# A router with the weights as the stationary side, and the norm's weight applied after the gather

## The reference, cut to what matters

```python
xn = rms_norm(h, ffn_norm_g)
group_prob = softmax(xn @ w_rg + b_rg)                  # 4 groups
g_w, g_idx = top_k(group_prob, 1)
e_logits = (xn @ w_re + b_re).reshape(B, S, 4, 8)       # 32 experts
sel = e_logits of the chosen group
e_w, e_idx = top_k(softmax(sel), 2); e_w = e_w / sum(e_w)
cw = one-hot of the two experts, times g_w * e_w         # S x 32
out = sum over e of (silu(xn @ w_gate[e]) * (xn @ w_up[e]) * cw[:, e]) @ w_down[e]
h = h + out; return rms_norm(h, final_norm_g)
```

## Time and profile before

| | us | share of the span |
|---|---|---|
| median of three runs | 1063.31 | |
| the profiled execution | 1062.29 | |
| its span | 1060.5 | |
| TensorE matmuls busy | 983.5 | 93% |
| TensorE weight loads busy | 752.2 | 71% |
| VectorE busy | 543.3 | 51% |
| ScalarE busy | 471.3 | 44% |
| GpSimd (POOL) busy | 8.0 | 1% |

### The profile page before, as it was taken

The page is one execution under the profiler, slowest core; times in us unless marked ns, Lnnn a source line. Parts: engine busy times, 40 slices in busy tenths (PEclk is TensorE's granted clock), DMA queues, the critical chain, the costliest instruction groups (busy, mean ns, idle before and its releaser), DMA issues.

```text
span 1060.5 us, 13681 instructions
## 1 busy us (share of the span) xinstructions
PE 983.5 (93%) x5518; PEld 752.2 (71%) x5518; DVE 543.3 (51%) x870; ACT 471.3 (44%) x753; POOL 8.0 (1%) x10
## 2 busy tenths in 40 slices
PE   5999998989999999999998879998948999999995
PEld 5879886877889999888887657797745444554542
DVE  4788785664666554555776654664361111111114
ACT  5488656555455344445554635353332222222222
POOL 0000000000000000000000000000020000000000
PEclk9999999999999999999999989999958999999998
DMA  9655464333554555436564423381564999999991
GB/s 297 233 165 179 134 237 161 118 119 121 192 175 159 200 197 190 168 122 208 171 194 129 170 80 120 123 313 47 169 228 178 383 393 395 394 393 396 393 367 42
DMA packets 106740, 224.02 MB, mean 211 GB/s; under 512 B 10041, under 2 KB 13874, under 8 KB 106674
## 3 DMA queue, kind: packets, MB, share of 16 engines
q1 hardware_dynamic: 103936, 218.13, 58.9%
q10 hardware_dynamic: 2738, 4.96, 1.4%
HBM read 222.03 MB, written 1.05 MB: 210 GB/s over the span
## 4 chain that ended last, share of the span: by engine, by line
PE 77%; DVE 12%; ACT 6%; issue 4%; DMA 1%; SPq 0%; ACTq 0%; DVEq 0%
PE pb L438 16%; PE pb L440 15%; PE pb L439 15%; PE pb L2217 11%; PE pb L2240 5%; PE pb L2199 3%; DVE wl L1406 3%; PE pb L2255 3%; ACT wh L885 2%; PE pb L496 1%; PE pb L567 1%; PE pb L637 1%; DMA raw<-in_w_in 1%; DVE BT L1460 1%; PE pb L577 1%
## 5 line engine op out<-in xcount | busy, mean ns | idle before, releaser
L1406 DVE TENSOR_TENSOR wl<-raw,wh 128x2048 fp32r<-128x2048 f32 (+4 forms) x115 | 251.6, 2194 | 145.3 <-ACT wh L885 145.2
L885 ACT ACTIVATE wh<-raw 128x2048 fp32r<-128x2048 f32 (+4 forms) x115 | 210.4, 1837 | 118.8 <-PE pb L440 116.5
L438 PE MATMUL pb<-wh,th 128*128 128x512 f32 (+3 forms) x636 | 254.6, 400 | 8.5 <-ACT RC L1283 4.3
L440 PE MATMUL pb<-wh,tl 128*128 128x512 f32 (+3 forms) x636 | 248.6, 391 | 0.0
L439 PE MATMUL pb<-wl,th 128*128 128x512 f32 (+3 forms) x636 | 248.6, 391 | 0.0
L438 PE MATMUL pb<-th,wh 128*128 128x256 f32 x544 | 156.4, 288 | 5.6 <-DVE wl L1406 5.6
L440 PE MATMUL pb<-th,wl 128*128 128x256 f32 x544 | 154.5, 284 | 0.0
L439 PE MATMUL pb<-tl,wh 128*128 128x256 f32 x544 | 154.2, 284 | 0.0
L438 PEld LDWEIGHTS pb<-wh,th 128*128 128x128 f32 x636 | 122.5, 193 | 37.7 <-issue 12.1
L440 PEld LDWEIGHTS pb<-wh,tl 128*128 128x128 f32 x636 | 122.2, 192 | 26.1
L439 PEld LDWEIGHTS pb<-wl,th 128*128 128x128 f32 x636 | 122.7, 193 | 23.5
(11 more groups left out here) (342 smaller groups left out, 1123.8 us busy)
## 6 DMA issues: line engine op xcount, KB each, us to landing
raw<-in_w_in SPq DMA_DIRECT2D x32, 1024.0 KB, 5.1
raw<-in_w_up SPq DMA_DIRECT2D x16, 1024.0 KB, 5.5
raw<-in_w_down SPq DMA_DIRECT2D x16, 1024.0 KB, 4.9
raw<-in_w_exp_gate SPq DMA_DIRECT2D x20, 512.0 KB, 9.6
raw<-in_w_exp_up SPq DMA_DIRECT2D x20, 512.0 KB, 11.3
raw<-in_w_exp_down SPq DMA_DIRECT2D x10, 1024.0 KB, 13.8
raw<-in_w_xkv SPq DMA_DIRECT2D x8, 1024.0 KB, 5.1
mwh<-in_w_exp_gate SPq DMA_DIRECT2D x14, 512.0 KB, 10.3
```

Of the source, the lines that this page charges most:

```text
L438: PE.matmul(o, lh, rh, start=start, stop=False, skip_group_check=True)
L440: return PE.matmul(o, ll, rh, start=False, stop=stop, skip_group_check=True)
L885: ACTE.activation(WH[i % NW][:, 0:kc * w], RAW[i % NRAW][:, 0:kc * w], ACT.Copy).then_inc(S["hi"], 1)
L1406: DVE.tensor_tensor(WL[i % NW][:, 0:kc * w], RAW[i % NRAW][:, 0:kc * w], WH[i % NW][:, 0:kc * w].bitcast(F), ALU.subtract).then_inc(S["lo" ...
```

## The change

- The router's unit is split into one tile: for each chunk of features 36 high columns and 36 low columns side by side. These 72 columns become the stationary side; the moving side is all 256 tokens, high half and then low half: 16 matmuls. (The product of low by low, which was left out, is now in it.) The result lies as 72 rows by 256 tokens. ScalarE copies it to S1, and two float32 matmuls with a matrix of two stacked identities ("fold") add the two halves and turn them back to tokens by 36.
- ScalarE does the first of the last two sums of squares ahead of the copies of chunks 4 to 7.
- The route works on all 32 experts: the logits of the groups not chosen get -1e30 added, the two maxima run over 32. Comparison and order become one instruction for each tile. The weights are made before the ranks are read; ranks are one higher, and so are the slots.
- Rows are split as they lie: ScalarE writes X times the factor as the high half, VectorE makes the low half inside the sparse branch. The norm's weight is applied by ScalarE while it copies the gathered columns (two activations of 256 columns with a per-partition factor in place of one of 512). POOL has nothing left to do here, and the broadcast load of the weight is gone; a load of 8 values per partition at the start replaces it.
- The gather reads its stationary side with a step of 8 elements, and the first gather takes the high halves, then the choosing, then the low halves.

```diff
+            PE.wait_ge(S["lo"], ROUTER + 1)
+            both = v3(WH[ROUTER % NW], 8, 72)
+            for k in range(8):
+                PE.wait_ge(*turned("ffn")(k))
+                for i, x in enumerate((TH[0], TL[0])):
+                    m = PE.matmul(PB[b0][0:72, 0:256], both[:, k, :], chunk(x, k), start=(k == 0 and i == 0), stop=(k == 7 and i == 1), ...)
+            m.then_inc(S["used"], 1)
+            PE.wait_ge(S["logits"], 1)
             for t in range(2):
-                for k in range(8):
-                    m = pe_mm3(PB[banks[t]][:, 0:36], TH[0][:, c], TL[0][:, c], hi[:, k, :], lo[:, k, :], k == 0, k == 7)
+                m = PE.matmul(PB[b1][:, 36 * t:36 * t + 36], S1[0:72, 128 * t:128 * t + 128], cst("fold", 36)[0:72, :], ...)
...
+            act_resid_squares("w_xo_2", 1, (0,))
             act_turn("ffn", range(4, 8), "ffn_norm_g_2", 0)
-            act_resid_squares("w_xo_2", 1)
+            act_resid_squares("w_xo_2", 1, (1,))
+            act_done(("router", 0), 0)
+            ACTE.activation(S1[0:72, 0:256], PB[banks_of(("router", 0))[0]][0:72, 0:256], ACT.Copy).then_inc(S["logits"], 1)
             ACTE.wait_ge(*scaled("ffn"))
             for t in range(2):
-                ACTE.activation(v3(S1, 2, 1024)[:, t], Xv[:, t], ACT.Copy, scale=rs_of["ffn"][:, t:t + 1]).then_inc(S["xs_scaled"], 1)
+                ACTE.activation(v3(XN[0], 2, 1024)[:, t], Xv[:, t], ACT.Copy, scale=rs_of["ffn"][:, t:t + 1]).then_inc(S["xn_hi"], 1)
...
-                POOL.tensor_tensor(s, s, FB[:, :], ALU.mult).then_inc(S["xs_gain"], 1)
-            POOL.tensor_tensor(XN4[1][:, 0], by_chunks[:, 0], XN4[0][:, 0].bitcast(F), ALU.subtract).then_inc(S["xn_lo0"], 1)
...
+            dve_then(DVE.tensor_scalar(off, og, -1.0, -NEG, ALU.add, ALU.mult))
+            dve_then(DVE.tensor_tensor(el..., L3[:, :, 4:36]..., off..., ALU.add))
+            dve_first_max(el, 32, o1, ma, 4, v_e, q_e)
+            dve_then(DVE.scalar_tensor_tensor(el, o1, NEG, el, ALU.mult, ALU.add))
+            dve_first_max(el, 32, o2, mb, 4, v_e, q_e)
+            DVE.tensor_tensor(e2, mb, ma, ALU.subtract).then_inc(S["route_e"], 1)
+            DVE.tensor_tensor(v3(mk, 2, 32), o1, o2, ALU.add).then_inc(S["mask_d"], 1)
...
                 for i in parts:
                     for k in range(2):
                         for t in range(2):
-                            l = XN[i][:, 1024 * t + 128 * (2 * r + k):1024 * t + 128 * (2 * r + k) + 128]
+                            l = v3(XN[i], 2, 1024)[:, t, 2 * r + k::8]
...
             def pe_sparse():
+                for r in range(4):
+                    pe_gather(0, r, (0,))
                 pe_choose(0)
                 for r in range(4):
-                    pe_gather(0, r)
+                    pe_gather(0, r, (1,))
...
-                ACTE.activation(XG[q % 2][:, 512 * r:512 * r + 512], gather_bank(q, r)[:, :], ACT.Copy).then_inc(S["g_x"], 1)
+                for k in range(2):
+                    ACTE.activation(chunk(XG[q % 2], 2 * r + k), gather_bank(q, r)[:, 256 * k:256 * k + 256], ACT.Copy,
+                                    scale=gffn[:, 2 * r + k:2 * r + k + 1]).then_inc(S["g_x"], 1)
...
             def dve_sparse():
                 dve_select(0)
+                for t in range(2):
+                    DVE.wait_ge(S["xn_hi"], t + 1)
+                    DVE.scalar_tensor_tensor(lo, Xv[:, t], rs_of["ffn"][:, t:t + 1], hi.bitcast(F), ALU.mult, ALU.subtract).then_inc(S["xn_lo"], 1)
```

More of the change, by code:

```diff
@@ L27 @@
 ROWS2 = [("q_norm_g_2", 3), ("kv_norm_g_2", 2), ("pool_scale_2", 4)]
-CONSTS = [("ident", 128), ("mask1", 384), ("mask2", 384), ("rope", 128), ("inv", 16), ("order", 12),
-          ("count", 64), ("slots", 64), ("upper", 128), ("ones", 128)]
+CONSTS = [("ident", 128), ("mask1", 384), ("mask2", 384), ("rope", 128), ("inv", 16), ("order", 36),
+          ("count", 64), ("slots", 64), ("upper", 128), ("ones", 128), ("fold", 36)]
 def offsets(rows):
@@ L61, in constants @@
     c[:, at["order"]:at["order"] + 4] = 4 - np.arange(4)
-    c[:, at["order"] + 4:at["order"] + 12] = 8 - np.arange(8)
+    c[:, at["order"] + 4:at["order"] + 36] = 32 - np.arange(32)
     for g, w in enumerate((2, 4, 8, 16)):
         c[:, at["count"] + 16 * g:at["count"] + 16 * g + 16] = 1.0 / np.minimum(np.arange(16) + 1, w)
-    c[:, at["slots"]:at["slots"] + 64] = np.arange(64)
+    c[:, at["slots"]:at["slots"] + 64] = np.arange(64) + 1
     c[:, at["upper"]:at["upper"] + 128] = q < k
     c[:, at["ones"]:at["ones"] + 128] = 1.0
+    for j in range(2):
+        c[36 * j:36 * j + 36, at["fold"]:at["fold"] + 36] = np.eye(36, dtype=np.float32)
     return c
@@ L146 @@
      "mlp_x", "ple_x", "zt", "pooled", "pool_mm", "pool_hi", "pool_lo", "cs_arg", "cs", "kr", "krope2", "qrope2", "kc",
-     "t2_mm", "t2", "xs_mm", "xmax", "xexp", "xprob", "xt_mm", "xt", "xv_mm", "xo_hi", "xo_lo", "xs_scaled", "xs_gain",
-     "route_e", "mask_d", "rank_mm", "flag", "rank", "weights", "xn_hi", "xn_lo0", "xn_lo1",
+     "t2_mm", "t2", "xs_mm", "xmax", "xexp", "xprob", "xt_mm", "xt", "xv_mm", "xo_hi", "xo_lo", "xs_scaled", "logits", "fold_mm",
+     "route_e", "mask_d", "rank_mm", "flag", "rank", "weights", "xn_hi", "xn_lo",
      "sel", "ch_mm", "ch", "g_mm", "g_x", "rise_t", "rise_g", "over_mm", "ht_mm", "ht", "down_mm", "yy_hi", "yy_lo", "spread",
@@ L354, in att_val, with raw_of, hi_of, lo_of @@
             return VM[:, t, h, :] if n >= 4 else KV[:, t, 256 + 64 * (h // 4):256 + 64 * (h // 4) + 64]
+        ROUTER = U["router", 0, 0]
+        def raw_of(i):
+            kc, w = shape_of(i)
+            return v3(RAW[i % NRAW], kc, w) if i == ROUTER else RAW[i % NRAW][:, 0:kc * w]
+        def hi_of(i):
+            kc, w = shape_of(i)
+            return v3(WH[i % NW], kc, 2 * w)[:, :, 0:w] if i == ROUTER else WH[i % NW][:, 0:kc * w]
+        def lo_of(i):
+            kc, w = shape_of(i)
+            return v3(WH[i % NW], kc, 2 * w)[:, :, w:2 * w] if i == ROUTER else WL[i % NW][:, 0:kc * w]
         def load(i):
@@ L856, in pe_main @@
             turn_x("ffn", "w_xo_2", range(4, 8))
-            i = U["router", 0, 0]
-            hi, lo, _ = pe_weights(i)
-            banks = banks_of(("router", 0))
+            PE.wait_ge(S["lo"], ROUTER + 1)
+            both = v3(WH[ROUTER % NW], 8, 72)
+            b0, b1 = banks_of(("router", 0))
             PE.wait_ge(*freed(("router", 0)))
-            for t in range(2):
-                for k in range(8):
-                    if t == 0:
-                        PE.wait_ge(*turned("ffn")(k))
-                    c = slice(k * 256 + t * 128, k * 256 + t * 128 + 128)
-                    m = pe_mm3(PB[banks[t]][:, 0:36], TH[0][:, c], TL[0][:, c], hi[:, k, :], lo[:, k, :], k == 0, k == 7)
[L867 to L873, removed]
+            for k in range(8):
+                PE.wait_ge(*turned("ffn")(k))
+                for i, x in enumerate((TH[0], TL[0])):
+                    m = PE.matmul(PB[b0][0:72, 0:256], both[:, k, :], chunk(x, k), start=(k == 0 and i == 0), stop=(k == 7 and i == 1),
+                                  skip_group_check=True)
+            m.then_inc(S["used"], 1)
+            PE.wait_ge(S["logits"], 1)
+            PE.wait_ge(S["d_const"], 16)
+            for t in range(2):
+                m = PE.matmul(PB[b1][:, 36 * t:36 * t + 36], S1[0:72, 128 * t:128 * t + 128], cst("fold", 36)[0:72, :], start=(t == 0),
+                              stop=True, skip_group_check=True)
+            m.then_inc(S["fold_mm"], 1)
+            PE.wait_ge(S["mask_d"], 1)
+            for a, b, l, r, go, end in ((0, 64, U_, mk[:, 0:64], True, False), (32, 64, ONE, mk[:, 0:32], False, True),
+                                        (64, 96, ONE, mk[:, 0:32], False, False), (64, 96, ONE, mk[:, 32:64], False, True)):
+                m = PE.matmul(PB[1][:, a:b], l, r, start=go, stop=end, skip_group_check=True)
             m.then_inc(S["rank_mm"], 1)
@@ L907, in act_square, with act_resid_squares @@
             ACTE.activation(junk, src, ACT.Square, accum_out=ssq[name][:, n:n + 1]).then_inc(S["square"], 1)
-        def act_resid_squares(name, b):
-            for t in range(2):
+        def act_resid_squares(name, b, tiles=(0, 1)):
+            for t in tiles:
                 ACTE.wait_ge(*evicted((name, b), t + 1))
@@ L1726, in build @@
         v_a, q_a = v3(rt(8), 2, 4), rt(2)
[L1727 to L1736, removed]
+        og, gm, eg, pg = v3(rt(8), 2, 4), rt(2), v3(rt(8), 2, 4), rt(2)
+        off = v3(rt(8), 2, 4)
+        el, v_e, o1, o2 = [v3(rt(64), 2, 32) for _ in range(4)]
+        ma, mb, q_e, e2 = rt(2), rt(2), rt(2), rt(2)
+        mk, rank, cw = rt(64), rt(64), rt(64)
         most, flag = rt(1), rt(1).bitcast(I32)
         wa, wb = rt(2), rt(2)
-        cw = se
         def b3(ap, n):
@@ L1778, in dve_route @@
[L1778 to L1796, removed]
-            dve_then(DVE.scalar_tensor_tensor(rank, PB[1][:, 0:64], 1.0, mk, ALU.add, ALU.mult))
-            dve_after()
```

(23 more changed lines are left out.)

107 lines of the change are left out of this document (48 added, 59 removed).

## The result

The changed kernel takes 1078.14 us in the median (1077.64 to 1081.34, 4 runs), against 1063.95 for the kernel before (4 runs): ratio 1.0142, interval [1.0126, 1.0158]. The forecast was 1049.0, faster. The changed kernel is slower, by 15.4 us of span (1075.9 for 1060.5; the profiled execution's own time is 1077.72).

What follows compares the result with a forecast made beforehand. TensorE was taken to bound the kernel, with one hole, the router; the expert loop would keep its 236.5 us. Starting TensorE 13.6 us earlier, plus 0.1 us at the start, gave 1048.8, stated as 1049.0; range 1045.5 to 1056.

Steps and rivals of the forecast that it cites:

- Steps 1 and 2: Router: product and fold give logits at 775.3; norm's factor, later, at 776.05; L1760 starts 4.2 us earlier.
- Step 3: Route, logits to mask: 4.45 us instead of 9.0, with POOL's operations gone; TensorE ranks at 780.5.
- Steps 4 and 5: Rank 1.9 us, covering the weights; branch 0.75 us after the flag; TensorE starts at 784.5, 13.6 us earlier.
- Step 6: First gather: same 32 matmuls and choosing, kept at 7.53 us; the weight on ScalarE's copies hidden.
- The cover for the low halves: First gather: VectorE's low-half passes done by 788.5 at the latest, before TensorE wants them at 789.2.
- Where the expert loop could pay: Gather's stepped stationary loads, 32 + 224 matmuls: rows disagree on a cost; without one the sum stands.
- rival B: Expert loop: stepped loads capped at the lower rate, gathers 0.215 apart, 21 us, 1070, slower; 9% (milder cap 5%).
- Rival C: Expert loop: transfers don't move with TensorE, so only 8.3 us of slack can be won: 1054; 5%.
- D: TensorE stays low longer, or VectorE's branch takes 2.07 us: gain 10 to 12, 1050.3 to 1052.5; 12%.
- E: Router hole doesn't close (POOL not the cause, or new waits cost as much): 2.1 + 0.8 us stay, 1052; 3%.

Runs made afterwards that it cites:

- pool_on: contig with POOL put back, multiplying the two halves of X (result unused) from the folded logits on: 1055.27 us, ratio 0.9927 to the kernel before.
- turn8: The kernel before with the eight transposes of the memory reading their input with a step of 8 elements: 1063.55 us, ratio 1.0006.
- contig: The changed kernel with the halves written reordered, so the gather's stationary side is contiguous, its new matmul order kept: 1049.09 us, ratio 0.9879 to the kernel before.
- the old order: contig with the first gather ordered as in the kernel before (choosing first, then high and low halves in turn): 1052.27 us, ratio 0.9902.

## Why the prediction was wrong

- **Steps 1 and 2 held.** Fold done at 774.9 (775.3 said), factor and logits at 775.9 and 776.0 (776.05 said).
- **Step 3 held**, 0.4 us short: from L1762 to L893 4.9 us for 4.45. The sum's terms as written add up to 4.64, not 4.45. The 0.25 us that 4.64 still lacks lies in the pairs of comparisons with order. They don't overlap: L1750 took 0.41 us for both on 32 elements, so the second comparison costs a full step and not the 0.09 us that the sum had as an estimate, and there are three such pairs. That POOL was behind the slow steps is shown by pool_on.
- **Steps 4 and 5 held.** Rank 1.92 us; weights done at 782.4, before the rank's end near 782.8; VectorE's next instruction 0.72 us behind the flag (0.75 said), its load began at 783.3. The gather started at 784.76, 784.5 said.
- **Step 6 failed** in its first words, "same 32 matmuls": 9.4 us for 7.53. They were no longer the same: their loads had the step. The cover for the low halves held (done at 787.1, wanted at 789.95), and no matmul waited for ScalarE's copies.
- **"Where the expert loop could pay" is the step that failed.** It named the stepped load and its bound as rival B (0.215 a matmul, 21 us, 1070, slower) and gave it 9%, so the term for the loop stood at nothing in the sum. The cap turned out at 0.234, past that bound: 25.8 us in the loop, 1.8 in the first gather. The bound assumed that a stepped load is no slower than a contiguous one at the lower clock; sixteen stepped gather matmuls took 4.04 to 4.25 us there (0.25 to 0.27 each) for 0.215, so it is. Two faults led to 9%. First, the row that outweighed the others was of another kind of load: a transposed one, which by turn8 pays a third of the price at the upper clock; and it was at the lower clock, where its price does not show at all. Second, ScalarE's row, L1372 at 4.02 us for 2.19 with the same step, was a sign that a reader can pay for steps of 32 bytes, and 256 loads hung on it. The loss had no upper edge in the sum: the range ended at 1056.
- **Rival C** fell, as contig shows: with the loop 13.7 us earlier it took the same 236.5 us, so the transfers moved with TensorE. **D** happened in part: the lower clock lasted about 3 us longer in the changed kernel's first gather, and fell once more behind it, for about 1 us together; VectorE's branch did not take its 2.07 us. **E** did not happen. The shares of the rivals, 66 to 5%, add up to 105%.
- The rest of the sum was right: with the step undone the time is 1049.1 (1048.8 in the sum), and the first expert matmul starts at 791.9 (792.0 said).

## What to carry to other kernels

Price an operand's layout at its reader in the loop, not only at its writer: reordering cost ScalarE and VectorE under 2 us each, once and beside other work, and saved TensorE about 28 us. A row stands for an operation only if it shares its kind of load, its step and its clock; if the nearest row differs in one of these and the operation runs 256 times, the outcome is as wide as the two rows that disagree, and a chance of 9% is too sure. Where POOL works beside a chain of tiny VectorE steps, look for steps that end when POOL's instruction does. And before two traces are compared for a microsecond, count both from an instruction that they share: the medians gave POOL 6.2 us and the old order 3.2, the traces 4.0 and 1.8.

## What was not expected of the hardware

- A float32r weight load with a step of 32 bytes lasts 0.33 to 0.34 us at either clock, and with 16 bytes 0.33 in the median (contiguous or 8 bytes: 0.19 at the upper, 0.33 at the lower). At the lower clock the duration hardly shows the step, but the distance of the matmuls does: 0.25 to 0.27 us for 0.215.
- ScalarE and VectorE pay for reading by the same step: two 128x1024 passes took ScalarE 2.19 us plain and 4.16 with single elements 32 bytes apart (3.43 us for pairs, in eight instructions of 256 columns), VectorE 2.47, 4.16 and 3.25.
- Fifteen matmuls in idle time kept the granted clock at 1.00 through the hole, where it had been 0.50 from about 777 to 790.5 (contig); the rank then took 1.08 us for 1.91.
